# GpSimd's order of scatters and weighing, and ScalarE's index copies, in the expert blocks of a decoder layer

## The reference

```
x  = x + g1 * rglru_mixer(modulate(rmsnorm(x, norm1_g), sh1, sc1))
hn = modulate(rmsnorm(x, norm2_g), sh2, sc2)
gates = the two largest router probabilities in the best group, made to sum to 1
act = silu(hn @ w_gate[e]) * (hn @ w_up[e]) * gates[e]      # for the two experts e of a token
x  = x + g2 * sum over e of (act @ w_down[e])
out = rmsnorm(x, final_norm_g)
```

## Time and profile before

| | us |
|---|---|
| median of 3 runs | 1300.38 (1300.13 to 1301.42) |
| the profiled execution | 1304.35 |
| its span in the trace | 1302.7 |
| busy: PE, DVE, ACT, POOL | 1096.4, 786.8, 631.4, 640.3 |

### The profile page before, as it was taken

One profiled execution on the slowest core, in us unless ns is written; L12 is line 12 of the kernel. 1 busy time (PEld: TensorE's weight loads), 2 busy tenths in 40 slices (PEclk: granted clock), 3 DMA queues, 4 the chain that ended last, 5 costly groups with the idle time before them and its releaser, 6 DMA issues. The chain is left out here.

```text
span 1302.7 us, 19169 instructions
## 1 busy us (share of the span) xinstructions
PE 1096.4 (84%) x4704; PEld 835.5 (64%) x4705; DVE 786.8 (60%) x1154; ACT 631.4 (48%) x928; POOL 640.3 (49%) x642
## 2 busy tenths in 40 slices
PE   1368999999999998389999981686989989999991
PEld 0256778787787786278888861564656666666660
DVE  6884667567667674535777767244555655556640
ACT  1464676676667566412222221234556656556641
POOL 0695626437246250022677667033646656565663
PEclk9999999999999999589999985697989999999995
DMA  8546244353344212661455537538668776778741
GB/s 303 179 99 202 82 134 117 116 161 105 109 133 149 97 56 90 213 225 66 162 178 204 201 121 273 177 112 290 231 243 284 273 270 232 255 261 280 257 137 65
DMA packets 143738, 232.60 MB, mean 179 GB/s; under 512 B 33728, under 2 KB 101312, under 8 KB 143056
## 3 DMA queue, kind: packets, MB, share of 16 engines
q1 hardware_dynamic: 108688, 128.20, 30.4%
q0 software_dynamic: 23632, 62.49, 13.4%
q10 hardware_dynamic: 11376, 41.42, 9.0%
HBM read 177.45 MB, written 91.31 MB: 206 GB/s over the span
## 5 line engine op out<-in xcount | busy, mean ns | idle before, releaser
L1631 PE MATMUL po<-w_dn,e_ah 128*128 (+1 forms) x312 | 147.8, 618 | 30.6 <-issue 20.4
L1610 PE MATMUL pl<-w_hi,e_xh 128*128 (+1 forms) x312 | 141.1, 452 | 15.7 <-DVE e_xl L1532 10.7
L1332 POOL TENSOR_TENSOR e_ob<-e_obs,e_fg 128x1024 f32<-128x1024 f32 x39 | 93.6, 2401 | 90.2 <-ACT e_idx_o L1438 77.0
L1165 PE MATMUL po<-wo_hi,b_yh 128*128 128x512 f32 x256 | 106.1, 414 | 27.6 <-DVE wo_lo L979 27.6
L1612 PE MATMUL pl<-w_hi,e_xl 128*128 (+1 forms) x312 | 125.2, 401 | 0.0
L1611 PE MATMUL pl<-w_lo,e_xh 128*128 (+1 forms) x312 | 124.6, 399 | 0.0
L1631 PEld LDWEIGHTS po<-w_dn,e_ah 128*128 128x128 f32 x312 | 58.5, 198 | 93.2 <-issue 92.9
L543 DVE SCALAR_TENSOR_TENSOR XB<-xu,conv_w,XB 128x512 f32<-128x512 f32 x96 | 91.6, 954 | 42.1 <-ACT XB L413 38.4
L636 PE MATMUL px<-hT_hi,wx_hi 128*128 128x512 f32 x256 | 101.8, 397 | 5.1 <-DVE wx_lo L477 5.1
L636 PE MATMUL pg<-hT_hi,wg_hi 128*128 128x512 f32 x256 | 104.2, 407 | 0.0
L1166 PE MATMUL po<-wo_lo,b_yh 128*128 128x512 f32 x256 | 102.3, 400 | 0.0
(11 more groups left out here) (266 smaller groups left out, 2639.7 us busy)
## 6 DMA issues: line engine op xcount, KB each, us to landing
e_xg<-hn_slots ACTq DMA_DIRECT2D x40, 512.0 KB
e_xa<-x_slots ACTq DMA_DIRECT2D x39, 512.0 KB, 4.4
stg<-in_ada_w_dram POOLq DMA_DIRECT2D x32, 512.0 KB, 4.2
w_raw<-in_moe_w_down_dram SPq DMA_DIRECT2D x16, 1024.0 KB
w_raw<-in_moe_w_gate_dram SPq DMA_DIRECT2D x32, 384.0 KB
w_raw<-in_moe_w_up_dram SPq DMA_DIRECT2D x32, 384.0 KB
n_ada<-in_ada_w_dram SPq DMA_DIRECT2D x16, 512.0 KB, 4.9
n_x<-in_x_dram SPq DMA_DIRECT2D x16, 512.0 KB, 3.3
```

The source lines that it names most:

```text
L1165: nc.tensor.matmul(po[u][:, hcols], yh[u][:, tok], wo_hi[:, k, hcols], start=(k == 0), stop=False)
L1332: nc.gpsimd.tensor_tensor(ob[:], obs[:], fg[:], ALU.mult).then_inc(out_ready, 1)
L1610: nc.tensor.matmul(gu[:], xh[:, tok], hi, start=(k == 0), stop=False)
L1631: last = nc.tensor.matmul(dst, ah[:, k * P:(k + 1) * P], rows, start=(k == 0), stop=(k == KF - 1))
```

## The change

On GpSimd `scatter_acc` and `root` of block i+1 go ahead of `weigh` and `scatter_out` of block i. On ScalarE `index_out` moves from behind `scale_row` to the end of the block, behind `high_w` and `index_acc`; the row numbers are read by `slot_rows` at the head of a block, ahead of `square`, and handed to `load_x` and `load_h`; and at the start of the stage `high_x(0)`, `tanh(0)` and `high_x(1)` go ahead of the wait for the scatters of x and of `load_x(0)`.

```diff
             for b in range(2):
+                scatter_acc(b + 1)
+                root(b + 1)
                 weigh(b, b == 0)
                 scatter_out(b)
-                scatter_acc(b + 1)
-                root(b + 1)
             with pool.Fori(2, nless + 1) as i:
+                scatter_acc(i + 1)
+                root(i + 1)
                 weigh(i)
                 scatter_out(i)
-                scatter_acc(i + 1)
-                root(i + 1)
...
-            def load_h(b):
+            def load_h(b, row0=None):
...
-                row0 = slot_rows(act, b)
...
             load_h(0)
+            act.wait_ge(w["tabled"], 1)
+            nless = blocks_less(act)
+            high_x(0, slot_rows(act, 1))
+            row0 = slot_rows(act, 2)
+            tanh(0)
+            high_x(1, row0)
             act.wait_ge(w["sent_x"], 96)
             load_x(0)
-            act.wait_ge(w["tabled"], 1)
-            nless = blocks_less(act)
-            high_x(0)
-            tanh(0)
-            high_x(1)
...
             with act.Fori(LEAD, nless) as i:
+                rows = slot_rows(act, i + 1), slot_rows(act, i + 4)
                 square(i)
                 high_a(i + 1)
-                load_x(i + 1)
+                load_x(i + 1, rows[0])
                 tanh(i + 2)
-                high_x(i + 3)
+                high_x(i + 3, rows[1])
                 scale_row(i)
-                index_out(i)
                 high_w(i + 2)
                 index_acc(i + 1)
+                index_out(i)
```

More of the change, by code:

```diff
@@ L1389, in load_h, with load_x @@
                 act.dma_start(xg[:], dr["h"][ds(row0, P), :]).then_inc(gathered, 16)
-            def load_x(b):
+            def load_x(b, row0=None):
                 if isinstance(b, int) and b == 0:
@@ L1401, in load_x, with high_x @@
                 act.dma_start(xa[:], dr["x2"][ds(row0, P), :]).then_inc(xa_in, 16)
-            def high_x(b, more=True):
-                if more:
-                    load_h(b + 1)
+            def high_x(b, row0=None):
+                if row0 is not None:
+                    load_h(b + 1, row0)
                 act.wait_ge(turned, b + 1)
@@ L1456, in expert_scalar @@
             load_h(0)
+            act.wait_ge(w["tabled"], 1)
[4 more added lines that the diff above has]
+            high_x(1, row0)
             act.wait_ge(w["sent_x"], 96)
             load_x(0)
-            act.wait_ge(w["tabled"], 1)
-            nless = blocks_less(act)
-            high_x(0)
-            tanh(0)
-            high_x(1)
             high_w(0, True)
             high_a(0)
+            row0 = slot_rows(act, 3)
             tanh(1)
-            high_x(2)
+            high_x(2, row0)
             act.wait_ge(rec_in[0], 16 * EARLY)
@@ L1471, in expert_scalar @@
             for b in range(LEAD):
+                rows = slot_rows(act, b + 1), slot_rows(act, b + 4)
                 square(b, b == 0)
                 high_a(b + 1)
-                load_x(b + 1)
+                load_x(b + 1, rows[0])
                 tanh(b + 2)
-                high_x(b + 3)
+                high_x(b + 3, rows[1])
                 scale_row(b, b == 0)
-                index_out(b, b == 0)
                 high_w(b + 2)
                 index_acc(b + 1)
+                index_out(b, b == 0)
             act.wait_ge(rec_in[1], 16 * (MAXB - EARLY))
             with act.Fori(LEAD, nless) as i:
+                rows = slot_rows(act, i + 1), slot_rows(act, i + 4)
                 square(i)
                 high_a(i + 1)
-                load_x(i + 1)
+                load_x(i + 1, rows[0])
                 tanh(i + 2)
-                high_x(i + 3)
+                high_x(i + 3, rows[1])
                 scale_row(i)
-                index_out(i)
                 high_w(i + 2)
                 index_acc(i + 1)
+                index_out(i)
+            rows = slot_rows(act, nless + 1), slot_rows(act, nless + 2)
             square(nless)
             high_a(nless + 1)
-            load_x(nless + 1)
+            load_x(nless + 1, rows[0])
             tanh(nless + 2)
             scale_row(nless)
-            index_out(nless)
             high_w(nless + 2)
             index_acc(nless + 1)
+            index_out(nless)
             square(nless + 1)
             high_a(nless + 2)
-            load_x(nless + 2)
+            load_x(nless + 2, rows[1])
             scale_row(nless + 1)
```

## The result

The kernel after takes 1350.62 us in the median of four runs (1348.54 to 1354.11), beside 1300.45 us (1300.13 to 1301.42) for the kernel before on the same chip: 1.0387 times as long [1.0361, 1.0413], or 50.2 us more. Predicted were 41 us more, from a ring of waits that takes TensorE's place as the bound. The profiled execution took 1352.33 us with a span of 1350.7 us.

A forecast was written before the change was run, and what follows sets the result against it. TensorE bounds the kernel before at 10.05 us a block; a 12.03 us ring of waits replaces it over 35 blocks, 39.7 us more, plus 1.3 at the start: +41.0 on the 1300.38 us median, 1341 us, range 1305 to 1375.

The forecast's parts named there:

- the ring: Expert stage, GpSimd and ScalarE: square, root, weigh, output's scatter, landing, index_out, reads, next square in sequence, 12.03 us a block.
- square to the output's issue: First stretch of the turn: 1.33 to the root's start, root 1.8, weigh 2.5, gap to the issue 0.86 us.
- issue to the index copy: Output scatter's issue to its landing, put at 3.5 us, the middle between other transfers' times; called the weakest number.
- index copy to the next square: On ScalarE: index_out 0.2 us, then the loop's end and two reads of row numbers, 1.84 us.
- the signs that the prediction named: Squares steadily 11 to 13 us apart, copy or square released by the landing, root waiting for square, sum not for its scatter.
- Part 2: GpSimd's and ScalarE's new order makes a 12.03 us cycle of waits against TensorE's 10.05: 39.7 us more over 35 blocks.
- The rival of a landing in the weights' traffic: Output's transfer meets SyncE's weight loads: landing 4.7 us, turn 13.2 us, kernel 1383 us; chance 0.13.
- a falling clock: TensorE idles 2 us a block and its clock drops: 15 us a block, some 1440 us; chance 0.02.
- Part 1: On GpSimd the sum's scatter goes first: some 13 us gained if nothing else changed, at most 21.7; nothing left of it.
- about 2.9 us, not 4: Gain in one shown block from issuing the sum's scatter first, if that scatter now takes the long issue itself.
- Part 3: Stage's start: first copy some 6 us sooner, covered by late third-expert weights, worth 0; GpSimd's extra steps before weigh(1), 1.3 us.
- Part 4: End of the stage: from the last square on the same chain of work as before, change 0.

The follow-up runs named there:

- new order alone: Kernel before with only GpSimd's loop order changed (sum's scatter and root ahead of weigh and output's scatter), ScalarE as before: 1452.59 us, 1.1166.
- index copies on GpSimd: Kernel before with both index copies moved from ScalarE to GpSimd, and GpSimd's loops in the changed order: 1300.22 us, 0.9974.
- the other order on GpSimd: Kernel before with GpSimd's loop as weigh(i), scatter_acc(i+1), scatter_out(i), root(i+1): 1424.57 us, 1.0988.
- the cut: Kernel after with index_out(i-1) moved behind high_a(i+1), a place reached after the square: 1319.45 us, 1.0133.
- the late reads: Kernel after with the row numbers in the loops read inside load_x and load_h again: 1334.08 us, 1.0259.
- the sixth experiment: Kernel before with the two scatters of GpSimd's loop swapped, so the output's scatter stands directly behind the sum's, ahead of the root: 1424.57 us, 1.0988.
- the ninth experiment: Kernel before with both index copies moved from ScalarE to GpSimd, GpSimd's order otherwise as before: 1323.48 us, 1.0193.

## Why the prediction was right, step by step

**The bound changed hands, as forecast.** The steps of the ring in the mean over blocks 3 to 36, from the starts of the instructions, beside the forecast:

| stretch of the ring | predicted | after | before | new order alone |
|---|---|---|---|---|
| square to the output's issue | 6.49 | 6.49 | -0.97 | 7.22 |
| issue to the index copy | 3.5 | 4.37 | 7.39 | 4.13 |
| index copy to the next square | 2.04 | 1.41 | 4.48 | 3.66 |
| turn | 12.03 | 12.27 | 10.90 | 15.0 |

The negative number is the whole matter: before, the output's scatter was issued 0.97 us ahead of the square of its block and needed nothing of it, so that its landing and the copy had all of TensorE's block to hide in. In the kernel after it hangs on the square, and the three stretches add up. Of the signs that the prediction named, the squares 11 to 13 us apart, the root that waits for the square, and the copy that waits for the landing came in most blocks and not in each: 22 of 35, 23 and 20. The squares weren't at a steady pace either, but 10.1 to 15.6 us apart. The sum still waits for its own scatter, half as long.

**Part 2, the sum of the ring.** The four steps from the square to the issue came out to the hundredth in their sum, and that is luck in part: the root started 1.54 us after the square and not 1.33, since in 11 of 34 blocks it follows the sum's scatter and not the square, and `weigh` took 2.31 us with its start and not 2.5. Two other terms were mis-sized, against each other. From the issue to the copy 3.5 us were put, between two rows of other transfers, and 4.37 measured; the reads with the copy were put at 2.04 from the start of the stage and measured 1.41. Together this is 8.6 us over 35 blocks. That the two errors offset each other is luck: the first alone would have made it 30 us. The whole difference of the profiled executions, 48.0 against the forecast 41.0, adds up from these 8.6, from -3.7 at the start (2.4 us gained where 1.3 were to be lost) and 2.1 at the end.

The step from issue to copy was also too simple. I had ScalarE's other work hide in the ring. It doesn't in 10 of 34 turns, where the copy comes behind `scale_row`, `high_w` and `index_acc` and the landing is already there. These turns don't need the transfer at all, and they still run through square, root and `weigh`: so the ring of the forecast has a second way beside the landing, nearly as long. In a block in which ScalarE converts weights, a landing under some 3.2 us would bring nothing.

**The traffic.** The rival of a landing in the weights' traffic (a ring of 13.2 us) is there in single turns, as in the one of 14.3 us above, and not in the mean: the landing is 3.92 us where the rival put 4.7. In the last turns, with no loads of weights beside it, it is 3.44 to 3.49 us, so by this what the transfer met on its way cost some 0.5 us in the mean; no run isolates it.

The Trainium skill (DMA: Bandwidth & Descriptors, "Anatomy of one DMA — SWDGE (gpsimd) path") would have made the landing 3.2 us for 512 KB, 2.0 of them fixed, by an estimate from its figure. The undisturbed turns at the end come near it: a landing of 3.44 to 3.49 us with rows, and of 2.19 to 2.57 us in the run without them. By the page's figure the ring would have come out shorter than it was, because in the mean the transfer meets traffic, the copy starts 0.17 us after the landing, and ScalarE's own work holds some of the turns.

**The clock.** I gave a falling clock a chance of its own as a collapse, and it came as a small term instead. Busy time by stretch (us, PE, PEld, DVE, ACT, POOL, granted clock, DMA share, GB/s), first after, then before:

```profile
887.00:1317.00 430.00, 370.21 (x1430) 248.42 (x1430) 220.78 (x249) 222.99 (x371) 213.57 (x245) 0.95 0.64 222
```

```profile
889.00:1271.00 382.00, 355.42 (x1430) 242.74 (x1430) 220.83 (x249) 223.08 (x370) 224.82 (x245) 0.98 0.72 249
```

The same 1430 matmuls take 370.2 us in place of 355.4, at a mean granted clock of 0.95 for 0.98. VectorE's and ScalarE's busy times agree to 0.1 us: nothing was added to the work, and the 48 us are waits. TensorE's products grew by 0.4 us a block, which lies within the 2.2 us that the turn of 12.28 us leaves beside its 10.05.

**Part 1, the sum's scatter first.** Expected was a gain of up to 13 us that the ring swallows. The wait it was to remove did fall, from 31.4 to 14.9 us, and TensorE got nothing of it. The long issue went over to the sum's scatter, as the prediction said: in the kernel before 19 of the output's issues met `w_lo` on VectorE and took 1.58 us in the mean, up to 2.62; in the kernel after all 34 take 1.09 us, and 16 issues of the sum that meet `w_lo` take 1.71 us in the mean, beside 0.98 for the others. The rule of the Trainium skill (SBUF — State Buffer, "SBUF: two separate sides") that the prediction names for this speaks of copies, and `w_lo` is a subtraction of two tiles; the trace agrees in the effect, and no run isolates the cause. The prediction's "about 2.9 us, not 4" doesn't come out of its rows: an issue of 2.62 us in place of 1.25 leaves 1.5 us of the 2.9. With the ring away (index copies on GpSimd) it fell to 10.7 us and the rows of x became late next, as named. There the whole kernel gained 0.26%, or 3.4 us, with an interval from 7.4 us of gain to 0.7 of loss, less than 13; what the copies cost on GpSimd isn't separated from it.

**Part 3, the start.** Right in its cover, nearly so in its size: the first copy 7.4 us sooner, the wait for weights 4.95 us longer, 2.4 us left over at the third square where I had said nothing. The edit alone changes the time by 0.0002 [-0.0036, 0.0041]. The 1.3 us for GpSimd's two extra steps ahead of `weigh(1)` can't be found among these.

**Part 4, the end.** Forecast was 0, measured are 2.1 us. The step between the last two squares was right (10.66 us against 10.89). The chain behind the last square isn't the same as before: GpSimd's order puts `weigh` and the output's scatter of the block ahead in front of the last root, and they came late, so that the root started 2.4 us later after its square. The 2.4 us gained at the start hide this in the total, which is chance.

**What the prediction didn't see.** It took ScalarE's edit as a mere help to GpSimd's. That edit closes a ring of its own (12.2 us), which the whole change happens to open again. The forecast didn't depend on it, but my first two expectations did, and the other order on GpSimd fell to the same oversight. I had looked for what a moved step waits for, and not for everything that stands behind it in its queue. What stays open is why opening one ring so regularly gave only part of its length back: in the cut, of 0.82 us a turn, the next ring is named; for the late reads I can only say that the two other stretches grew by a quarter of a microsecond each, the landing among them.

## What to carry to other kernels

Where two in-order queues wait for each other over small tiles (an index row, a freed buffer), write down the whole ring before moving a step: every instruction that stands behind each wait, the landing, the wake, the reads; then compare the sum with the pace of the busiest engine. Rings lie close together (11.5, 11.8, 12.2 and 14.4 us here around a pace of 10.9), so opening one earns only the distance to the next, and an edit may be worth +152 or -23 us depending on who does a copy of 128 numbers. With the copy on the engine that also waits for the transfer and issues the next one, no other queue stands still for it; here that paid only together with the new order, and in the old order it cost 1.9%. Where two paths into the same step are nearly as long, as the landing and ScalarE's work are here, shortening one shows little of its price.

## What the runs showed of the hardware

- An indirect scatter from GpSimd of 128 rows of 4 KB landed 3.44 to 3.49 us after its issue began where no weights were being loaded, and 2.19 to 2.57 us with its rows skipped. Over all blocks single ones took up to 6.2 and 6.4 us, and the means were 3.92 and 3.45 us.
- An output scatter issued directly behind the sum's landed after 7.6 us in the mean (the sixth experiment), against 3.9 us in the kernel after.
- Every issue of an indirect scatter that took longer than 1.10 us, up to 2.62 us, met VectorE's work on `w_lo`; without it the issues took 0.98 us (the sum's) and 1.09 us (the output's). This is read from blocks 3 to 36 of both kernels; no run isolates it.
- The two reads of row numbers on ScalarE cost 1.03 us per turn in the mean when they stand on the ring (1.41 us to the square against 0.38). In a turn whose copy waited, the idle time ahead of the square is 1.38 us, and not the 1.84 us that the start of the stage shows.
- A scatter that waits for an instruction of GpSimd itself starts 0.85 to 0.89 us after it (the turn of the ring above, the block of the ninth experiment), and one that finds its wait met by another engine starts 0.30 us after the instruction ahead of it. So a copy of 0.2 us on GpSimd costs its scatter more in the gap than in the work. The output's scatter of the ninth experiment's block is an exception, with 2.08 us while VectorE is on `w_lo`.
